# Forming half of each modulation output's terms on VectorE, and adding them on TensorE with a column of ones

## The reference, cut to what matters

```python
D = 1024
c_act = jax.nn.silu(c)
for l in range(DEPTH):
    mod = c_act @ ada_w[l] + ada_b[l]
    sh1, sc1, g1, sh2, sc2, g2 = [m[:, None, :] for m in jnp.split(mod, 6, axis=-1)]
    h = x * (1.0 + sc1) + sh1
...
    mod_l = jax.nn.silu(c) @ w_mod[layer] + b_mod[layer]
    mod_c = jax.nn.silu(c_ctx) @ w_mod[layer] + b_mod[layer]
```

## Time and profile before

| what | value |
|---|---|
| median of 3 runs | 4456.01 us (4453.72 to 4457.52) |
| the profiled execution's own time | 4459.17 us |
| its span, first to last instruction | 4457.4 us |
| TensorE's mean granted clock, as a share of 2.4 GHz | 0.683 |
| TensorE matmul busy | 1810.2 us, 41% |
| VectorE busy | 3055.7 us, 69% |
| mod0, first weight load issued to copy of the last row group | 13.72 to 103.36 us |
| mod1, the same | 597.1 to 686.92 us |
| mod20, the same | 976.21 to 1065.85 us |

### The profile page before, as it was taken

One profiled execution on the slowest core, in us unless ns is written; L12 is line 12 of the kernel. 1 busy time (PEld: TensorE's weight loads), 2 busy tenths in 40 slices (PEclk: granted clock), 3 DMA queues, 4 the chain that ended last, 5 costly groups with the idle time before them and its releaser, 6 DMA issues. The chain is left out here.

```text
span 4457.4 us, 32759 instructions
## 1 busy us (share of the span) xinstructions
PE 1810.2 (41%) x9516; PEld 1336.0 (30%) x9516; DVE 3055.7 (69%) x5169; ACT 797.7 (18%) x1477; POOL 1362.5 (31%) x820
## 2 busy tenths in 40 slices
PE   7668985988977864000003600000166561000001
PEld 1657933963735750000003300000054561000000
DVE  0456514721165268999997899999843658999997
ACT  0334412521232241000001200000032241000000
POOL 0000000000000032666664266666400021666663
PEclk9868997999975686555556855555577785555555
DMA  7313552545200126999995499999630031999996
GB/s 256 106 38 132 179 200 102 171 155 196 70 0 1 38 85 272 422 421 420 415 415 231 165 422 422 417 417 418 275 122 3 1 121 70 422 421 418 420 414 257
DMA packets 168885, 1061.95 MB, mean 238 GB/s; under 512 B 18604, under 2 KB 22444, under 8 KB 57664
## 3 DMA queue, kind: packets, MB, share of 16 engines
q0 software_dynamic: 110592, 805.36, 43.7%
q1 hardware_dynamic: 58176, 255.33, 16.4%
HBM read 1059.56 MB, written 1.05 MB: 238 GB/s over the span
## 5 line engine op out<-in xcount | busy, mean ns | idle before, releaser
L1651 POOL DMA_INDIRECT peer_gather_raw<-in_peer_uv,peer_experts x768 | 1247.9, 1625 | 903.0 <-DVE peer_gather_out L1678 453.2
L1660 DVE CUSTOM_DVE_ANT_0 peer_gather_raw<-peer_gather_raw,peer_rows 128x1024 f32<-128x1024 f32 x768 | 910.8, 1222 | 126.8 <-DMA peer_gather_raw<-in_peer_uv,peer_experts 126.7
L1678 DVE SCALAR_TENSOR_TENSOR peer_gather_out<-peer_gather_raw,peer_gather_gelu,peer_gather_out 128x1024 f32<-128x1024 f32 x762 | 928.3, 1281 | 6.8
L1703 PE MATMUL peer_gather_acc<-all_constants,peer_gather_out 128*128 128x128 f32 x48 | 11.0, 423 | 2052.2 <-DVE peer_gather_out L1678 2052.2
L1515 POOL TENSOR_TENSOR peer_keys_lo<-peer_pick_wq_raw,peer_keys_hi 128x1024 fp32r<-128x1024 f32 x48 | 114.4, 2387 | 2138.4 <-ACT peer_keys_hi L1474 2138.4
L1703 PEld LDWEIGHTS peer_gather_acc<-all_constants,peer_gather_out 128*128 128x128 f32 x48 | 9.8, 227 | 2052.5 <-DVE peer_gather_out L1678 2052.5
L1696 ACT ACTIVATE peer_gather_gelu<-peer_gather_score 128x4 f32<-128x4 f32 x192 | 39.4, 205 | 1903.1 <-DVE peer_gather_score L1660 1903.1
L449 PE MATMUL mod_acc<-mod_weights,mod_act_c 128*1 128x512 f32 (+1 forms) x576 | 254.2, 604 | 44.8 <-DMA mod_weights<-in_ada_w 31.7
L124 PE MATMUL ffn_up_acc<-first_h_hi,ffn_up_hi 128*128 128x256 f32 x704 | 201.0, 286 | 36.5 <-DVE ffn_up_lo L617 36.5
L124 PE MATMUL ffn_up_acc<-first_h_lo,ffn_up_hi 128*128 128x256 f32 x704 | 200.6, 285 | 0.0
L124 PE MATMUL ffn_up_acc<-first_h_hi,ffn_up_lo 128*128 128x256 f32 x704 | 200.5, 285 | 0.0
(11 more groups left out here) (475 smaller groups left out, 4881.0 us busy)
## 6 DMA issues: line engine op xcount, KB each, us to landing
mod_weights<-in_ada_w SPq DMA_DIRECT2D x48, 1024.0 KB, 4.7
in_up_raw<-in_w_up SPq DMA_DIRECT2D x88, 512.0 KB, 4.0
mod_weights<-in_w_mod SPq DMA_DIRECT2D x24, 1024.0 KB, 4.7
peer_pick_wq_raw<-in_peer_wq SPq DMA_DIRECT2D x48, 512.0 KB, 3.3
peer_select_next_raw<-in_w_mod SPq DMA_DIRECT2D x24, 1024.0 KB, 5.8
ffn_down_raw<-in_w_down SPq DMA_DIRECT2D x32, 704.0 KB, 5.2
peer_gather_raw<-in_peer_uv,peer_experts POOLq DMA_INDIRECT x768, 11.2
in_in_raw<-in_ab_w_in SPq DMA_DIRECT2D x17, 512.0 KB, 3.3
```

What stands on the lines that cost most here:

```text
L1651: nc.gpsimd.indirect_dma_start(raw[:, n % ring].rearrange("p c d -> p (c d)"), None, uv_rows, bass.IndirectOffsetOnAxis(index[:, i, e:e + ...
L1660: nc.vector.tensor_tensor_reduce(raw[:, n % ring, 0, :], raw[:, n % ring, 0, :], rows[:, i, :], 1.0, 0.0, ALU.mult, ALU.add, score[:, e, i ...
L1678: nc.vector.scalar_tensor_tensor(out[:, i, :], raw[:, n % ring, 1, :], gelu[:, e, i:i + 1], out[:, i, :], ALU.mult, ALU.add).then_inc(s_su ...
L1703: ins = nc.tensor.transpose(acc[:, k, i * P:(i + 1) * P], out[:, i, k * P:(k + 1) * P], ident)
```

## The change

In the three stages of `modulation`, the second piece of each group (chunks 4 to 7) no longer goes through TensorE. VectorE multiplies each of its four chunks, 128 x 512, by the condition's value of each partition and adds the products up, in `part_sum`, 128 x 512 for each condition. So each partition holds its own four terms of each output. One more TensorE matmul per condition then sums over the 128 partitions, and adds the result to the PSUM bank that already has the sum of chunks 0 to 3: its stationary operand `pick[:, j, :]` is 128 x n with ones in column j and zeros elsewhere, and its moving operand is `part_sum`. ScalarE copies the group when that is done (`s_joined`).

The order of additions changes, and the arithmetic stays float32. The loops are written out in place of `each_chunk`. SP still issues a load when its slot is free: the first piece's when TensorE has used it (`s_used`), the second's when VectorE has summed it (`s_summed`). `Steps` (L63) puts a wait between one step of VectorE's sum and the next, because each reads what the one before wrote; with two conditions there is one wait for each pair of instructions.

```diff
@@ -414,43 +414,48 @@
     n = c.shape[2]
     groups = 6 * D // 512
     half = KD // 2
     with Stage(nc, name) as st:
         act_c = st.sb("act_c", [P, KD, n])
         wt = st.sb("weights", [P, 4, half, 512])
+        part_sum, pick = st.sb("part_sum", [P, 2, n, 512]), st.sb("pick", [P, n, n])
         rows = st.sb("rows", [n, groups, 512])
         acc = st.ps("acc", [P, 4, 512])
         cols = st.ps("cols", [P, 6 * KD, n])
         s_loaded = [st.sem(f"loaded{r}") for r in range(4)]
-        s_silu, s_used, s_row, s_cols, s_bias = (st.sem(k) for k in ("silu", "used", "row", "cols", "bias"))
+        s_silu, s_used, s_row, s_cols, s_bias, s_pick, s_term, s_summed, s_joined = (
+            st.sem(k) for k in ("silu", "used", "row", "cols", "bias", "pick", "term", "summed", "joined"))
         with nc.Block() as block:
             @block.sync
             def _(sp):
-                def fetch(u, slot, turn):
-                    if not isinstance(u, int) or u >= 4:
-                        sp.wait_ge(s_used, u - 3)
-                    sp.dma_start(wt[:, slot], weights[bass.ds(u, 1)].rearrange("a p k c -> p (a k) c")).then_inc(s_loaded[slot], 16)
-                for u in range(4):
-                    fetch(u, u, 0)
-                each_chunk(sp, 4, 2 * groups - 4, 4, fetch)
+                for g in range(groups):
+                    for i in range(2):
+                        slot = 2 * (g % 2) + i
+                        if g >= 2 and i == 0:
+                            sp.wait_ge(s_used, g - 1)
+                        if g >= 2 and i == 1:
+                            sp.wait_ge(s_summed, g - 1)
+                        sp.dma_start(wt[:, slot], weights[2 * g + i]).then_inc(s_loaded[slot], 16)
 
             @block.tensor
             def _(pe):
                 pe.wait_ge(s_silu, 1)
-
-                def body(g, b, turn):
-                    pe.wait_ge(s_row, g + 1)
-                    for i in range(2):
-                        slot = 2 * b + i
-                        pe.wait_ge(s_loaded[slot], turn * 16 + 16)
-                        for k in range(half):
-                            ins = nc.tensor.matmul(acc[0:n, b, :], act_c[:, i * half + k, :], wt[:, slot, k, :],
-                                                   start=(i == 0 and k == 0), stop=(i == 1 and k == half - 1))
-                        ins.then_inc(s_used, 1)
-                each_chunk(pe, 0, groups, 2, body)
-                pe.wait_ge(s_row, groups + 2)
+                pe.wait_ge(s_pick, n + 1)
+                for g in range(groups):
+                    if g >= 2:
+                        pe.wait_ge(s_row, g - 1)
+                    pe.wait_ge(s_loaded[2 * (g % 2)], 16 * (g // 2 + 1))
+                    for k in range(half):
+                        ins = nc.tensor.matmul(acc[0:n, g % 2, :], act_c[:, k, :], wt[:, 2 * (g % 2), k, :], start=(k == 0), stop=False)
+                    ins.then_inc(s_used, 1)
+                    pe.wait_ge(s_summed, g + 1)
+                    for j in range(n):
+                        ins = nc.tensor.matmul(acc[0:n, g % 2, :], pick[:, j, :], part_sum[:, g % 2, j, :], start=False, stop=(j == n - 1))
+                    ins.then_inc(s_joined, 1)
+                pe.wait_ge(s_row, groups)
                 for m in range(6 * KD):
                     ins = nc.tensor.transpose(cols[:, m, :], rows[:, m // 4, m % 4 * P:(m % 4 + 1) * P], ident[0:n, 0:n])
                 ins.then_inc(s_cols, 1)
@@ -458,15 +463,35 @@
             @block.scalar
             def _(act):
                 nc.scalar.activation(act_c[:], c, ACT.Silu).then_inc(s_silu, 1)
-                act.sem_inc(s_row, 2)
-
-                def body(g, b, turn):
-                    act.wait_ge(s_used, g * 2 + 2)
-                    nc.scalar.activation(rows[:, bass.ds(g, 1), :], acc[0:n, b:b + 1, :], ACT.Copy).then_inc(s_row, 1)
-                each_chunk(act, 0, groups, 2, body)
+                for g in range(groups):
+                    act.wait_ge(s_joined, g + 1)
+                    nc.scalar.activation(rows[:, g, :], acc[0:n, g % 2, :], ACT.Copy).then_inc(s_row, 1)
 
             @block.vector
             def _(dve):
+                term = Steps(dve, s_term)
+                nc.vector.memset(pick[:], 0.0).then_inc(s_pick, 1)
+                dve.wait_ge(s_pick, 1)
+                for j in range(n):
+                    nc.vector.memset(pick[:, j, j:j + 1], 1.0).then_inc(s_pick, 1)
+                dve.wait_ge(s_silu, 1)
+                for g in range(groups):
+                    if g >= 2:
+                        dve.wait_ge(s_joined, g - 1)
+                    slot = 2 * (g % 2) + 1
+                    dve.wait_ge(s_loaded[slot], 16 * (g // 2 + 1))
+                    for k in range(half):
+                        for j in range(n):
+                            scale, mine = act_c[:, half + k, j:j + 1], part_sum[:, g % 2, j, :]
+                            if k == 0:
+                                ins = nc.vector.tensor_scalar(mine, wt[:, slot, k, :], scale, None, ALU.mult)
+                            else:
+                                ins = nc.vector.scalar_tensor_tensor(mine, wt[:, slot, k, :], scale, mine, ALU.mult, ALU.add)
+                            if k < half - 1:
+                                term.done(ins)
+                        if k < half - 1:
+                            term.wait()
+                    ins.then_inc(s_summed, 1)
                 dve.wait_ge(s_cols, 1)
                 nc.vector.tensor_tensor(mods[:], cols[:], bcast(bias, n), ALU.add).then_inc(s_bias, 1)
                 dve.wait_ge(s_bias, 1)
```

## The result

The changed kernel takes 4417.76 us (median of four runs, 4400.51 to 4426.39), the kernel before 4456.77 in the runs beside it (4453.72 to 4459.60). The ratio is 0.9911, with a 95% interval of 0.9895 to 0.9926: 0.9% faster, not 1.2%. The forecast of 4401 was 17 us too low, and its upper end of 4416 was missed by 2 us. The profiled execution has its own time of 4426.39 us, 32.8 less than the 4459.17 of before.

What follows compares the result with a forecast made beforehand. TensorE was taken to bound the three modulation stages; loads would then bound mod0 and mod1. Gains of 2 x 22.5 + 10.1 = 55.1 us from 4456.0 gave 4400.9 us, range 4391 to 4416.

Steps and rivals of the forecast that it cites:

- 0.7 us to spare: mod0 and mod1: a load could land at 9.3 us and must at 10, so the DMA engines stay busy.
- could at 4.6 + 4.7 = 9.3: mod0 and mod1: slot freed 4.6 us after its piece landed, next load lands 4.7 us after issue.
- its 2.5 us from mod0: Time per load with several outstanding, from the first four loads landing between 18.5 and 26.0 us; 420 GB/s.
- the forecast for the last piece: mod0 and mod1: the last group's second piece lands 63.1 us after the first load's issue.
- VectorE's 2.8: mod0 and mod1: one multiply, three multiply-and-adds and the waits between them take 2.8 us per group.
- the tail of 1.15: Stage end: after VectorE's last sum, 0.43 + 0.59 + 0.13 us until the last row copy starts.
- The forecast's ring: mod20: VectorE, TensorE and loads tied by slot reuse, three groups in 18.0 us, 6.0 each; stage 79.5 us.
- mod20 gains more: Rival: mod20's loads overlap better, VectorE alone sets the step; stage 73 us, gain 16.6, kernel 4394 us; 10%.
- 5.0 us per load pair: mod0 and mod1: a group needs two loads of 2.5 us, the new bound; each stage 67.1 us.
- The clock falls: Rival: waits drop TensorE to 1.2 GHz in the three stages; 76 us slower, 4532 us; 6%.
- The loads do not overlap: Rival: each pair shows 2.2 us once, 7.2 us per one-condition group; kernel 4441 us; 6%.
- It doesn't do what it says: Rival: TensorE would wait for something taking the full 6.87 us per group; no chance of its own given.

Runs made afterwards that it cites:

- ring8: Changed kernel with eight weight slots in place of four, each load issued up to four groups ahead: 4396.20 us, ratio 0.9866.
- filler: Changed kernel plus two small unused TensorE matmuls per group ahead of the wait for VectorE: 4421.60 us, ratio 0.9919.
- n1_only: Changed kernel with mod20 back on the old function, so only mod0 and mod1 are changed: 4422.24 us, ratio 0.9915.
- ring6_strict: Changed kernel with six slots, but loads issued no earlier than with four: 4408.86 us, ratio 0.9889, the first time.
- late_join: Changed kernel, still four slots, with each group's joining matmul moved behind the next group's four matmuls: 4410.33 us, ratio 0.9883.
- ring6: Changed kernel with six slots in place of four and loads issued up to three groups ahead: 4394.07 us, ratio 0.9864.
- before_ring8: Kernel before the change with eight slots, loads issued up to eight ahead, all chunks on TensorE: 4458.65 us, ratio 1.0007.
- after_again: Changed kernel run again without any edit, in the session of the other experiments: 4421.42 us, ratio 0.9924.
- after_third: Changed kernel unaltered once more, beside the second run of six slots with late issue: 4417.37 us, ratio 0.9920.
- late_ring8: Changed kernel with eight slots and the joining matmul one group later: 4374.66 us, ratio 0.9838.
- ring6_strict_again: Second run of the changed kernel with six slots and loads issued no earlier than with four: 4422.29 us, ratio 0.9930.

## Why the prediction was wrong, point by point

**The step that failed** is this one: "So the DMA engines stay busy, with 0.7 us to spare." They are busy, but don't carry the 420 GB/s that this was to mean. The term behind it is the 4.7 us from issue to landing in "could at 4.6 + 4.7 = 9.3". The 4.6 us until TensorE frees the slot of a first piece came true (in mod0 3.8 to 5.0, and 6.6 once, at half clock), but from the fifth group on the load issued then lands 6.0 to 7.4 us after its issue, 6.9 on average. One of them:

```profile
L441 SPq DMA_DIRECT2D mod_weights<-in_ada_w x1: 328/328/328, 38.7 to 38.7; - x1
...
DMA to landing us min/median/max: 6.7/6.7/6.7
```

So a slot comes round after 4.6 + 6.9 = 11.5 us where 10 were needed, and since a round is two groups, a group takes about 5.7 us in place of 5.0. That is what the stage shows. The packets of the stretch from 30 to 70 us, by queue (packets, MB, share of 16 engines), before, after and in ring8:

```profile
q1 hardware_dynamic: 1698, 12.34, 88.0%
```

```profile
q1 hardware_dynamic: 2086, 15.19, 97.0%
```

```profile
q1 hardware_dynamic: 2312, 16.85, 101.2%
```

A packet takes 0.880 x 640 us / 1698 = 0.33 us before, 0.97 x 640 / 2086 = 0.30 after, and 1.012 x 640 / 2312 = 0.28 with the reserve, at the same mean size of 7.3 KB. So of the 10% that the rate lacks against ring8, 4 points are idle time and 6 slower packets.

The events of the trace show what this does to a load. It lands in 16 parts. Columns: first part, last part, their distance, and the last part's distance from that of the load ahead, in us from the span's start.

```
before   39.14  39.47   0.33   3.42
         42.63  42.92   0.29   3.45
after    38.06  39.61   1.55   2.48
         40.53  42.07   1.54   2.46
         43.28  45.42   2.14   3.35
         46.01  48.20   2.19   2.78
         49.28  50.65   1.38   2.45
         51.76  53.13   1.37   2.48
         54.34  56.47   2.12   3.34
         57.34  58.96   1.62   2.49
         59.81  62.73   2.92   3.77
ring8    39.33  39.83   0.50   2.48
         41.82  42.33   0.51   2.50
         44.30  44.82   0.52   2.49
```

After the change most loads land 2.5 us behind the one ahead, as forecast, but every few loads one is 0.9 to 1.3 us later. And the parts drift: the last is 1.4 to 2.9 us behind the first, and only the last frees VectorE or TensorE. From 31.26 to 76.11 us, 16 loads come 2.80 us apart on average, 5.6 per group. Before, at TensorE's pace of 3.4 us, the parts of mod0's loads were within 0.6. In ring8 the loads come 2.48 to 2.50 us apart with their parts within 0.5, up to 59.7 us. Then one, landed at 63.5, comes 3.8 us behind the one ahead and the drift is 1.7 to 1.8 too, but nothing waits so closely that the delay grows.

A single late load needs neither the change nor a thin reserve. The kernel before has one among the first four of mod20, issued together while VectorE does nothing: the third landed at 987.18, 3.76 us behind the second, its parts 1.55 apart.

```profile
L434 SPq DMA_DIRECT2D mod_weights<-in_w_mod x2: 424/424/425, 976.6 to 977.1; - x2
...
DMA to landing us min/median/max: 6.8/8.5/10.1
```

The prediction had read its 2.5 us from mod0, where none of the four was late (6.9 and 8.9 us for the same two loads).

The estimate had taken the 2.5 us from four loads issued together, and used it for loads issued in pairs as slots come free, with 0.7 us between "could land" and "must land". One delay of 0.9 uses that up. From then on the ring passes it on: the first load of the last group could be issued only at 74.6, of which the half clock of 69.7 to 73.1 us has up to 1.7, and landed 6.5 us later.

```profile
L441 SPq DMA_DIRECT2D mod_weights<-in_ada_w x2: 328/380/432, 74.6 to 75.0; - x2
...
DMA to landing us min/median/max: 6.5/7.7/8.8
```

Its second piece took 8.8 us and landed at 83.8, where the forecast for the last piece is 63.1 us from the first issue, 75.9 on this axis. With VectorE's 2.8 and the tail of 1.15 that gives 87.7; the copy started at 88.25.

The reserve decides by size. By the forecast's own reckoning four slots leave 0.7 us, and a third pair of slots adds one group, 5.0 us:

| kernel | reserve | mod0 / mod1, us |
|---|---|---|
| the changed kernel (three profiles), filler, n1_only, ring6_strict (two) | 0.7 | 73.3 to 77.5 |
| late_join | VectorE's sum no longer ahead of the first slot | 70.2 / 70.0 |
| ring6 | 5.7 | 67.6 / 66.8 |
| ring8 | 10.7 | 67.7 / 67.4 |

Shown are the missing reserve as the cause and the early issue as the cure. Why a load's parts drift and single packets take longer is open. It is common where few loads stand in the queue, but the late load of ring8 had five others behind it. And in mod0 of before_ring8, where VectorE reads nothing, loads issued only 5.9 and 4.9 us ahead of their landing still came 2.5 us behind the one ahead, with their parts within 0.4. So it isn't excluded that VectorE's reads help to spread the parts when the reserve is thin; no run measured that by itself.

**mod20.** The forecast's ring gave 6.0 us per group; in the first profile the stage averages 6.3 (331 GB/s against the 350 forecast), and its 10.1 us shrank to 6.2. That execution had one stretch at half clock here and two groups of 7.8 and 8.4 us. In after_again and after_third the stage takes 80.7 and 80.3 us, within 1.2 of the forecast's 79.5, so this part of the prediction was nearly right. The rival "mod20 gains more" assumed VectorE's step as the bound. It didn't happen in the changed kernel, but is what ring6 and ring8 do, 71.3 us against its 73. VectorE in mod20 of ring8 (start, us):

```profile
946.67 0.88 DVE L487 TENSOR_SCALAR mod_part_sum<-mod_weights,mod_act_c 128x512 f32<-128x512 f32 x2
947.59 4.32 DVE L489 SCALAR_TENSOR_TENSOR mod_part_sum<-mod_weights,mod_act_c,mod_part_sum 128x512 f32<-128x512 f32 x6
951.82 0.88 DVE L487 TENSOR_SCALAR mod_part_sum<-mod_weights,mod_act_c 128x512 f32<-128x512 f32 x2
```

A group takes 951.82 - 946.67 = 5.15 us, where 5.3 was forecast (the forecast's own sum, 0.88 + 3 x 1.42 + 0.1, is 5.24). TensorE's six matmuls, 5.15, are as near. The eight instructions alone last 2 x 0.485 + 6 x 0.751 = 5.48, so some of them overlap. The prediction had read the Trainium skill ("VectorE: DVE Perf Modes", The DRAIN you can't avoid) as excluding that. The same section of the Trainium skill adds that a next instruction that is not held starts earlier. So the Trainium skill leaves room for the overlap, and the trace, with 5.15 against 5.48, shows it.

**What was right.** The multiply 0.485 us (0.48 forecast), the multiply-and-add 0.751 (0.75), VectorE's busy time +128 us (+131), TensorE's 5 and 6 matmuls no longer the bound, VectorE waiting for a load in each one-condition group, and 192 passes less on TensorE (9516 to 9324). The stages reach 67 us once the loads keep up. Of the forecast 5.0 us per load pair nothing was wrong but the condition for it.

**The rivals.** *The clock falls:* in short stretches it did, at 0.50 for 3.4 us each, once or twice a stage, not two groups in five. The Trainium skill ("TensorE: Matmul & The Clock Gate", A second HAM failure mode) describes this swing; here it is rare, absent in after_again, after_third and filler. It costs up to 1.7 us each time, 7 to 8 us at most in the first profile, and without it 14 to 15 us of the gain are still missing. *The loads do not overlap:* it was right in its doubt about pairs issued as slots come free, and wrong in size. A one-condition group takes 5.6 us, between 5.0 and its 7.2. The forecast should have put that middle case into its sum. *It doesn't do what it says:* it does: the five or six matmuls and the four or eight VectorE instructions per group are there, and no group is as long as 6.87 us for that reason.

The range was too narrow for the same reason: it took in a few groups with a load late, at 2.2 us each, and nothing let one late load delay those behind it. That the median missed the range by only 2 us is no sign of a nearly right sum. One of its four times lies at the lower of two levels (last section), which has nothing to do with the forecast; the other three are at 4414.7 to 4426.4.

## What to carry to other kernels

A rate read from transfers that are issued together holds only as long as several stand in the queue. When a change makes the loads the bound, take the slack between "slot free" and "next load needed", and if it is below about one transfer (here 2.5 us), don't count on the full rate: 0.7 us of slack gave 380 of 422 GB/s. A third pair of slots (16 KB per partition here) with the earlier issue brought it back. Slots without the earlier issue gave nothing, and eight slots with it gave nothing in the kernel that TensorE bounded. And a time from issue to landing that was read from loads issued 3.4 us apart (4.7 us here) isn't that of loads issued in pairs (6.9).

## What the runs showed that was not expected

The times of one kernel lie on two levels. The changed kernel had 13 of 16 times at 4414.6 to 4426.9 us and three at 4398.0 to 4400.7; ring8 one at 4372.4 and four at 4395.8 to 4398.8. The profiles tell where the difference lies: in the window attention, about 1360 us into the kernel, which the change doesn't touch. After (4426.4 us), two windows of it:

```profile
1363.00:1411.00 48.00, 47.20 (x158) 36.69 (x159) 18.14 (x65) 16.39 (x56) 0.00 (x0) 0.50 0.00 1
1411.00:1446.00 35.00, 35.00 (x127) 29.27 (x126) 13.59 (x33) 10.80 (x26) 0.00 (x0) 0.50 0.00 1
```

ring8 (4372.4 us), the same two from its start:

```profile
1329.00:1377.00 48.00, 47.27 (x158) 36.78 (x159) 18.22 (x65) 16.46 (x56) 0.00 (x0) 0.50 0.00 1
1377.00:1412.00 35.00, 30.51 (x208) 26.25 (x208) 20.78 (x52) 18.44 (x44) 0.00 (x0) 0.99 0.01 1
```

The first 48 us are alike, at half clock with TensorE nearly always busy. Then the clock stays at 1.2 GHz in the one and TensorE is busy in all of the 35 us; in ring8 it is at 2.4 GHz, and 208 matmuls run in 30.51 busy us instead of 127 in 35. From the first matmul to the last transposes the stage takes 113.4 us in the one and 91.4 in the other:

```profile
1363.12 3.75 PE L996 MATMUL window_attention_scores<-mixab_qk 64*128 64x256 f32 x8 [5.60 <-PEq L50]
...
1476.48 0.47 PE L1027 MATMUL window_attention_back<-all_constants,window_attention_o_tok 128*128 128x128 f32 x1 [0.23 <-DVE window_attention_o_tok L1069]
```

```profile
1329.04 3.75 PE L996 MATMUL window_attention_scores<-mixab_qk 64*128 64x256 f32 x8 [5.60 <-PEq L50]
...
1420.39 0.47 PE L1027 MATMUL window_attention_back<-all_constants,window_attention_o_tok 128*128 128x128 f32 x1 [0.23 <-DVE window_attention_o_tok L1069]
```

22 us is the distance between the levels. All profiles with the stage at 91 us (ring8, after_again with 4400.7 us, late_ring8 with 4373.8) are of the lower level, all with 113 us of the upper. The kernel before stayed on the upper one in all its profiled and nearly all its timed executions; one time of 4433.8 us, among the 11 beside ring6_strict_again, may be the lower. What makes the clock rise in one execution and not in the next, and whether the change makes it more likely, is open. Compared on one level the kernels stand as their stages say: 4421 for the changed kernel, 4396 for ring8, ring6 and late_ring8, and 4400 against 4373 on the lower.
